# Attention of two transformer blocks on one core: query blocks taken in the order 0, 3, 1, 2, and three gated branches interleaved within a query block

## What is computed

```python
for l in range(2):                                  # first block
    y_a = sparse_indexed_attention(qa, ka, va, ...) # 8 heads of 64, chunk mask + top-128 mask + bias
    y_b = latent_attention(qb, kb, vb)              # 8 heads, queries and keys of 96 = 64 + 32, chunk mask
    x = x + (gate_a * (y_a @ w_proj_a) + gate_b * (y_b @ w_proj_b)) @ w_out
    x = x + (silu(gat) * val) @ w_down              # val, gat: a short convolution over h @ w_up
# second block
o_a   = mixer_dilated(...)                          # 8 heads
o_cmp = nsa_compressed_branch(...)                  # 8 heads, 31 compressed keys
o_slc = nsa_selected_branch(...)                    # 8 heads
o_win = nsa_window_branch(...)                      # 8 heads
o_b   = gate0 * o_cmp + gate1 * o_slc + gate2 * o_win
h = h + concat(o_a, o_b) @ w_out
h = h + (silu(h @ w_gate) * (h @ w_up)) @ w_down
```

## Time and profile before

| | |
|---|---|
| time before, median of 3 runs | 2794.61 us (2793.38 to 2798.28) |
| profiled execution, its own time | 2801.89 us |
| its span, first to last instruction | 2800.1 us |
| mean granted clock of PE | 0.939 of full |
| PE busy | 2531.1 us, 90% |
| POOL busy | 1874.1 us, 67% |
| DVE busy | 1329.6 us, 47% |
| ACT busy | 590.6 us, 21% |
| attention, pass 1 of section A | 275.8 to 379.4 us, PE busy 92.42 of 103.53 us |
| attention, pass 2 of section A | 1238.0 to 1344.9 us, PE busy 95.02 of 106.90 us |
| attention, section B | 2178.6 to 2347.0 us, PE busy 146.18 of 168.40 us |

### The profile page before, as it was taken

The page is one execution under the profiler, slowest core; times in us unless marked ns, Lnnn a source line. Parts: engine busy times, 40 slices in busy tenths (PEclk is TensorE's granted clock), DMA queues, the critical chain, the costliest instruction groups (busy, mean ns, idle before and its releaser), DMA issues. The chain is left out here.

```text
span 2800.1 us, 35444 instructions
## 1 busy us (share of the span) xinstructions
PE 2531.1 (90%) x11499; PEld 1856.8 (66%) x11499; DVE 1329.6 (47%) x2160; ACT 590.6 (21%) x1320; POOL 1874.1 (67%) x864
## 2 busy tenths in 40 slices
PE   5986989989999978889899899998889889899997
PEld 3663557757777755655677577776767556677776
DVE  4386553357525335855533673353411563542243
ACT  2212530023101122136200321111000563110001
POOL 4573248868788865632688687888578325688886
PEclk9997999989999989879999899999689989899999
DMA  5321012222223222200122222223453001222222
GB/s 159 98 75 38 2 38 91 87 66 93 85 90 90 90 76 91 68 31 1 53 90 90 68 90 83 92 88 90 105 174 97 16 1 38 68 93 94 90 94 79
DMA packets 62257, 214.61 MB, mean 77 GB/s; under 512 B 6401, under 2 KB 6529, under 8 KB 62129
## 3 DMA queue, kind: packets, MB, share of 16 engines
q1 hardware_dynamic: 54144, 195.06, 22.1%
q10 hardware_dynamic: 7984, 17.88, 2.4%
HBM read 210.75 MB, written 10.01 MB: 79 GB/s over the span
## 5 line engine op out<-in xcount | busy, mean ns | idle before, releaser
L422 PE MATMUL out_tile<-arena_r,w_hi 128*128 128x512 f32 x5418 | 1731.7, 401 | 0.0
L1494 POOL TENSOR_TENSOR w_hi<-weight_ring,cst 128x1024 fp32r<-128x1024 f32 x363 | 888.9, 2449 | 575.6 <-issue 462.6
L422 PE MATMUL out_tile<-arena_r,w_lo 128*128 128x512 f32 (+1 forms) x2709 | 1114.4, 411 | 160.8 <-DVE arena_r L1154 81.0
L422 PEld LDWEIGHTS out_tile<-arena_r,w_hi 128*128 128x128 f32 x5418 | 1043.2, 193 | 232.4
L1498 POOL TENSOR_TENSOR w_lo<-weight_ring,w_hi 128x1024 fp32r<-128x1024 f32 x363 | 898.5, 2475 | 28.5
L422 PEld LDWEIGHTS out_tile<-arena_r,w_lo 128*128 128x128 f32 x2709 | 521.0, 192 | 397.6 <-DVE arena_r L1154 95.9
L1136 DVE TENSOR_TENSOR x<-out_tile,x 128x512 f32<-128x512 f32 x72 | 49.8, 692 | 386.1 <-PE out_tile L422 386.1
L1512 POOL TENSOR_SCALAR work<-work,small 128x128 f32<-128x128 f32 (+1 forms) x80 | 53.9, 674 | 206.6 <-DVE small L1175 206.6
L915 ACT ACTIVATE work<-work,small 128x384 f32<-128x384 f32 (+4 forms) x256 | 134.3, 525 | 248.7 <-DVE small L1167 248.7
L1078 DVE CAST arena_r<-work 128x512 f32 (+2 forms) x94 | 172.6, 1836 | 13.5 <-issue 11.9
L1080 DVE TENSOR_TENSOR arena_r<-work,arena_r 128x512 f32 (+2 forms) x94 | 156.8, 1668 | 14.2 <-issue 12.1
(11 more groups left out here) (153 smaller groups left out, 1767.4 us busy)
## 6 DMA issues: line engine op xcount, KB each, us to landing
weight_ring<-stream SPq DMA_DIRECT2D x364, 512.0 KB, 3.5
bias_rows<-bias_kept ACTq DMA_DIRECT2D x3, 2556.0 KB, 19.8
strips<-bias_rows ACTq DMA_DIRECT2D x3, 2048.0 KB, 8.1
x<-x_t SPq DMA_DIRECT2D x4, 512.0 KB, 8.2
arena<-bias_rows ACTq DMA_DIRECT2D x1, 2048.0 KB, 9.3
out_t<-arena SPq DMA_DIRECT2D x8, 256.0 KB, 2.2
cst<-consts ACTq DMA_DIRECT2D x1, 820.0 KB, 9.5
arena<-spread ACTq DMA_DIRECT2D x1, 256.0 KB, 11.0
```

The lines of the kernel that those rows point to most:

```text
L422: ins = pe.matmul(out, l, r, start=start and n == 0, stop=stop and n == 2, **kw)
L1494: pool.tensor_tensor(w_hi[:, s % SPLIT, :].rearrange("p (w c) -> p w c", c=P), ring[:, s, :].rearrange("p (w c) -> p w c", c=P), ones.unsq ...
```

## The change

The query blocks are taken in the order 0, 3, 1, 2 in all kinds. In section B, the gated branches no longer run one after the other over all query blocks: within a query block they alternate "cmp", "sel", "win". Which item opens and which closes a group follows the new order (block 0 and block 2). A wait for the top-128 selection moves with the second item pair, which is now that of block 3.

```diff
 LAG_TURN, LAG_PV, SLOTS = 2, 3, 4
-ITEMS_1 = [(k, 2 * c + e, b) for k in "ab" for c in range(HEADS // 2) for b in range(QB) for e in range(2)]
-ITEMS_2 = [("A", 2 * c + e, b) for c in range(HEADS // 2) for b in range(QB) for e in range(2)]
-ITEMS_2 += [(k, 2 * c + e, b) for c in range(HEADS // 2) for k in ("cmp", "sel", "win") for b in range(QB)
+BLOCKS = (0, 3, 1, 2)
+ITEMS_1 = [(k, 2 * c + e, b) for k in "ab" for c in range(HEADS // 2) for b in BLOCKS for e in range(2)]
+ITEMS_2 = [("A", 2 * c + e, b) for c in range(HEADS // 2) for b in BLOCKS for e in range(2)]
+ITEMS_2 += [(k, 2 * c + e, b) for c in range(HEADS // 2) for b in BLOCKS for k in ("cmp", "sel", "win")
             for e in range(2)]
@@
 def opens(item):
-    return item[2] == 0 and item[0] not in ("sel", "win")
+    return item[2] == BLOCKS[0] and item[0] not in ("sel", "win")
@@
 def closes(item):
-    return item[2] == QB - 1 and item[0] not in ("cmp", "sel")
+    return item[2] == BLOCKS[-1] and item[0] not in ("cmp", "sel")
@@
-                    if (h, b) == (0, 1):
+                    if (h, b) == (0, BLOCKS[1]):
                         pe.wait_ge(selected, L * (QB - 1) + QB - 1)
```

## The result

| | before | changed |
|---|---|---|
| median of 20 runs | 2797.39 us (2793.38 to 2800.53) | 2806.31 us (2796.75 to 2810.52) |
| profiled execution, its own time | 2801.89 us | 2805.77 us |
| pass 1, pass 2, section B: first minimum to the next projection | 102.5, 102.7, 166.5 us | 102.6, 104.0, 168.9 us |

The ratio is 1.0033, with an interval of 1.0026 to 1.0040: the change makes the kernel 8.9 us slower. The stages above give just this: 0.1 + 1.4 + 2.4 = 3.9. Where the other 5 us are is shown by the experiment before_again.

A forecast was written before the change was run, and what follows sets the result against it. In attention's plain periods it took the chain through ACT's copies and PE's transposes, not PE's own work, to decide. Terms 12.7 - 1.0 - 1.5 - 8 + 0 = +2.2 us gave 2797 us, range 2785 to 2811.

The forecast's parts named there:

- plain kinds after the first period: Attention periods "a", "b" and "A": two PE waits each where there was one, +0.88, +0.51 and +1.10 us, +12.7 in all.
- first periods of the two passes: First period of each stage: fills the pipeline, so left out of the sum; counted only in the upper bound of 16.
- drains of the two passes: End of each stage: last item pair is block 2 instead of 3, so narrower work; -1.0 us, bounds 0 and -2.4.
- falls of the clock in "b": One slow "b" period in each pass; one of the two expected gone, -1.5 us, bounds 0 and -3.
- gated part: Gated branches of section B: half of the time at 1.2 GHz goes, -8 us, bounds 0 and -16.
- ACT's copy holds the odd transposes: Attention steps: POOL frees the even half of PE's transposes, ACT's copy of the pair before frees the odd half.
- rival 1: Attention transposes: ACT's copy does not hold them, only the scaling does; 22 us faster, 2772; chance 0.08.
- The walk through the period: Plain attention periods summed leg by leg, block 3 scores to the next: "A" 11.51 us, "a" 12.00, "b" 13.05.
- 0 for the new neighbours at an even clock: Gated part: interleaving costs nothing at an even clock, taken between +9 for new waits and -8 for hidden "cmp" steps.
- Rivals 1 and 2: First: only scaling holds the transposes, 2772, chance 0.08. Second: clock no longer falls in the gated part, 2789, chance 0.17.
- Rival 4: Plain kinds, steps of blocks 0 and 1 in "A" and "b": added waits cost clock too, +12, 2809; chance 0.15.
- Rival 3: Gated part: the clock falls there as long as before; 10 us slower, 2805; chance 0.16.

The follow-up runs named there:

- before_again: The kernel before once more, unchanged, in one execution for a second profile of it: 2796.22 us.
- order_only: Against the kernel before, the block order 0, 3, 1, 2 alone, gated branches still one after the other: 2805.51 us, ratio 1.0027.

## Why the prediction was right or wrong

It said 2797 us, 2.2 more than before, with a range of 2785 to 2811; measured were 2806.3, 8.9 more. The range of 26 us holds the time, and the sign is right, but the range of the sum itself, 2790 to 2804, does not hold it. Of the 9.5 us between 2797 and 2806.3, 2.8 come from the median of before (2794.6 of three runs, 2797.4 of twenty), and 6.7 are in the sum. The gated part is off by as much, 7 us; the other terms are off too, and their errors nearly cancel, which is luck. Against the second execution of before, with the drain of pass 1 taken without its fall, it is:

| term | predicted | in the traces |
|---|---|---|
| plain kinds after the first period | +12.7 | +9.4 |
| first periods of the two passes | 0 | +3.5 |
| drains of the two passes | -1.0 | -3.1 |
| falls of the clock in "b" | -1.5 | 0 |
| gated part | -8 | -0.8 |
| sum | +2.2 | +9.0, beside 8.9 measured |


- **ACT's copy holds the odd transposes: right.** This was the step on which the plain term rested, and rival 1 denied it. Copies made shorter, or moved ahead of the exponentials, take the loss away. A wait for two semaphores was put down to POOL in the earlier trace rows, and only the 0.11 us between the end of the copy and the odd half gave it away.
- **The walk through the period: right, a little high.** "A" was to be 11.51 us, "a" 12.00, "b" 13.05; they are 11.39, 11.83, 12.91. The eight legs of "A" are 1.34, 3.12, 0.26, 0.80, 1.49, 2.98, 0.37 and 1.03 in the timeline above (the sixth with the minimum of one period of 11.39 earlier), against 1.34, 3.11, 0.26, 0.80, 1.61, 3.00, 0.37 and 1.02. The leg that was off is the one over the split, for which the step of before (1.61) had been taken as it stood: there the split's first part began 0.24 us after the scores, here it begins 0.11 after them. The two waits stand before T(1) and T(0), as said, 0.72 + 0.61 = 1.33 us and 0.26 + 0.76 = 1.02 us for the 1.2 to 1.5 and about 1 of the prediction. In full flow the cost is 0.71, 0.37 and 0.98 us a period for 0.88, 0.51 and 1.10.
- **+12.7 for the plain kinds.** The periods give in each pass, from the second period on, +0.7, +0.7, +1.1 and three times +0.4, thus 3.7 for the seven periods that were counted as 4.7. "A" gives +1.0 for the first period, 0.2 for the second and twice 1.0, together 3.2 for 3.3. The sum is 10.6. In pass 2 the second period is shorter by 1.1 than in full flow, behind a first one of 11.15 us at a clock of 0.50, which leaves 9.4.
- **0 for the first periods.** They were left out of the sum because they fill the pipeline, and stood only in its upper bound. Against the second execution of before they cost 0.3 us in pass 1 (8.66 for 8.40) and 3.2 in pass 2 (11.15 for 7.92); the execution that the prediction read has 9.18 and 9.27.
- **-1.0 for the drain: too small.** From the start of the last "b" period to the split of its bank it was 377.52 - 358.51 = 19.01 us in pass 1 of before and is 378.41 - 360.97 = 17.44 now: -1.6, and in pass 2 17.45 for 19.14 and 18.97 in the two executions of before, where 0.3 to 0.8 was taken.
- **-1.5 for falls of the clock in "b": the falls were gone, but they were not the change's to remove.** Before again had none in a "b" period in either pass. Two of them were in the execution that the prediction read; a median hardly has them. This and the first periods are why the profiles differ by less than the medians.
- **-8 for the clock in the gated part: this is the step that failed.** From the first gated minimum to the last split the part took 127.90 us before and 127.16 after: -0.7. "I take half of the time at 1.2 GHz to go" was too much. It went from 54 us (four times 13.5) to some 38 (10.3, 3.4, 10.5, and 13.8 in the last stretch of 36.32 us at 0.81), so that less than a third of it went. Before, the clock fell once a period, each time for some 13.5 us; now there are eight falls in the four periods, five of 3.4 us and three of about 7. The price per us, 0.30, was too low: about 0.38. (By its own working it would be 3.9 us a period and not 4.1, since 13.65 us hold 2.0 us of waits and not 1.8; that changes little.) The fewer us and the higher price partly cancel, 16 x 0.38 = 6.1 us.
- **0 for the new neighbours at an even clock: failed with it.** Of the 6.1 us, 5.4 were spent again. At an even clock a gated period of the changed kernel is 28.02 - 3.4 x 0.38 = 26.7 us. For the one of before, which was never seen at an even clock, 30.66 - 13.5 x 0.38 = 25.5 is an estimate; with its own slope in the run with short copies (30.65 at 0.78, 28.45 at 0.88, so 0.33 per us) it is 26.2. That is 0.5 to 1.2 us a period, 2 to 5 in all. The first stretch has 1.5 more (32.08 less 10.3 x 0.38 is 28.2), whose cause stays open. Together they are 3.5 to 6.3 us, beside the 5.4. All of these are estimates that hang on the price. Since order_only, without the interleaving, has a gated part of 124.96 us, the interleaving on top of the order cost 2.2 us in these executions and gained nothing.
- **The rivals.** Rivals 1 and 2 did not come true: the copies hold, and the clock falls in each gated stretch. Rival 4 did not either. "A" has PE busy 9.04 of 11.39 us, 79%, and its clock is 1.00, as it is in each full plain period above. By the rule of the Trainium skill, "TensorE: Matmul & The Clock Gate", section "A second HAM failure mode: psum-queue depth-cycling", the added idle pieces should have cost clock; in the plain kinds the trace disagrees. In the gated part the falls became more and shorter, and no run shows whether the pauses bring them on. Rival 3, at 2805, is nearest in time, though the time at 1.2 GHz did shrink. Its chance (0.16) was too low beside the 0.44 for the sum.

That the interleaving alone gains 4.5 us and nothing on top of the new order is shown by the runs; why the clock falls in one and not in the other is not. The copy-first runs speak against a simple account by the groups of PE's program, since the same program had both outcomes.

## What to carry to other kernels

Where an instruction waits for two things, look at what ended just before each half of it (here 0.11 us), not only at the releaser that the view names. Before reordering items, look at the order inside the engine that drains them: moving a short copy ahead of an exponential that waits for a later step turned this order from 0.33% slower into 0.46% faster. Read a second execution of the kernel before, and take from the sum what only one of them has.

## What the runs showed of the hardware

- The first period of a pass is not repeatable: the same work took 9.18, 9.27, 8.40 and 7.92 us in two executions of the kernel before, at clocks of 0.61, 0.57, 0.69 and 0.74. In the changed one it took 8.66 us at 0.78 in pass 1 and 11.15 at 0.50 in pass 2, and the 11.15 came back in pass 2 of the four other profiled kernels with its order.
- In the gated part a microsecond at 1.2 GHz cost 0.38 us in three kernels and 0.32 to 0.45 in six others; PE waits for 4.7 of 26.85 us at a full clock.
- The same program of PE with the same work had gated clocks of 0.79, 1.00, 1.00 and of 0.74, 0.94, 0.79, when only the order of ACT's instructions differed (one profiled execution of each).
